# Third block's attention heads: the order of scores, transpositions and products, two heads apart

## The chip, the cores and the metric

The kernel runs on one core of a Trainium2 chip. The metric is the device time of one launch in microseconds (us), the median of several launches. Engines are named as in the profile: PE (TensorE, matrix products), DVE (VectorE), ACT (ScalarE), POOL (GpSimd), SP (the queue that starts most transfers).

## What is computed

The reference is a model of three parts on 256 tokens of width 1024: a retention layer and a sparse-attention layer, each followed by a mixture of experts, and then a block ("third block" in the kernel's order of stages) with two branches, a state-space branch and a dilated-window attention. The change touches only that attention, which has 12 heads of width 64; at this length each head's whole 256 x 256 matrix of scores is formed. Cut to what matters:

```python
scores = einsum('bdhine,bdhime->bdhinm', qs, ks) * (1.0 / sqrt(e))
scores = scores - slopes * dist          # dist is masked beyond the window
m = max(scores, axis=-1)
p = exp(scores - m)
den = sum(p, axis=-1)
o = einsum('bdhinm,bdhime->bdhine', p, vs) / den
lse = m + log(den)
```

In the same stretch of the program the input `xbc` of the state-space branch (3072 columns, 12 halves of a slab of 512 columns, 256 each) is projected, convolved over five taps and passed through silu. The two pieces of work are independent; the kernel pairs one attention head with one half-slab of `xbc`.

## The kernel before

The kernel is written engine by engine, each with its own instruction stream, and the order on an engine is the order of the code. Semaphores join them: `wait_ge` stands in an engine's stream and everything behind it on that engine waits too.

For one head `hd` the pieces are:

- S, the scores on PE (`att_scores`, matmul line L1204): two 64-row products into one bank of accumulation memory.
- L, on DVE: scores plus distance term into `a_S` (L2279), the largest value per row (L2283) and its scaled negative (L2284), which raises `att_max_ready`.
- E, on ACT: two exponentials with row sums (L1653) into `a_P`, which raise `att_exp_ready`.
- T, on PE: four 128 x 128 transpositions of `a_P` (`transpose4`, L853) into a bank; then the copy of that bank to `a_PT` by ACT (L1658).
- P, on PE: the products with the values (L1225) into a bank; then the copy to `a_o` by DVE (L2289).
- X, on PE: the projection of one half-slab of `xbc` (`xbc_half`, `split_columns`, 48 matmuls, L804). Weights are split in two parts: `high(q)` on ACT rounds a half-slab (L1407), `low(q)` on DVE forms the rest (L1829), and X waits for `low`. `high(q)` waits until PE has finished the half-slab two before it.
- On the side: ACT copies each finished pair of half-slabs to `c_raw` (L1666), DVE convolves (`conv(n)`, L2267 and L2269), ACT applies silu (`conv_out(n)`, L1645).

In the trace one f32 matmul of S or P stands as two rows (four rows for S, eight for P), one of T or X as one.

The four banks for such intermediate results are used in turn: bank number `b` may be taken when `b - 4` has been copied out (`take_aux`). On PE the loop before is, for each head, S, X, T, P. T waits for E of the same head, P for the copy of the transpositions, which begins when T ends.

Behind the 12 heads come the cumulative sums of the state-space branch (L1235, L1241) and the "gates" projection: four half-slabs, called G0 to G3 here, again L804. `high` of G2 waits for G0's end. Behind it, in the order of ACT and DVE, stand `low` of G2, the last convolution, `conv_out(11)`, the logarithm of the row sums (L1676), `high` and `low` of G3, and G3 waits for that.

Of the kernel before, what the change touches and what calls it, by code (L numbers as in the profile page):

```python
# [25 lines left out]
ACT = mybir.ActivationFunctionType  # L26
# [3 lines left out]
P = 128  # L30
T = 256
NT = T // P
# [20 lines left out]
NSA_H, NSA_G, DH = 16, 4, 64  # L53
# [5 lines left out]
ATT_H, ATT_PAT, ATT_HPP = 12, 3, 4  # L59
# [14 lines left out]
SL, PJ, AX, AR = {}, {}, {}, {}  # L74
# [77 lines left out]
def build(nc, x_tok, x_feat, slabs, experts_w, c_all, c_ret, c_nsa, c_ssd, c_att, w_pattn, ln_gb, out):  # L152
    ctx = ExitStack()
    with ctx:
# [378 lines left out]
        def wait_aux_out(eng, b):  # L533

            eng.wait_ge(aux_out[b % 4], b // 4 + 1)
# [17 lines left out]

        def nsa_ready(*name):
            return AR["nsa_att"] + NSA_BANK[name] + 1

        def aux(b):
            return bank(4 + b % 4)
# [212 lines left out]
        def _(pe):  # L771
# [9 lines left out]
            def take_aux(b):  # L781
                if b >= 4:
                    wait_aux_out(pe, b - 4)
                return aux(b)
# [64 lines left out]
            def transpose4(b, src):  # L849

                dst = take_aux(b)
                for q in range(4):
                    last = nc.tensor.transpose(dst[:, q * P:(q + 1) * P], src(q), ident)  # L853
                last.then_inc(aux_ready, 1)
# [343 lines left out]


            def att_scores(hd):  # L1200
                s = take_aux(AX["att"] + 3 * hd)
                half = slice(hd % 2 * DH, hd % 2 * DH + DH)
                for i in range(NT):
                    last = nc.tensor.matmul(s[:, i * T:(i + 1) * T], a_qkT[half, hd // 2, i * P:(i + 1) * P],  # L1204
                                            a_qkT[half, 6 + hd // 2, :], start=True, stop=True)
                last.then_inc(aux_ready, 1)

            def xbc_half(n):

                j = PJ["att"] + n // 2  # L1210
                split_columns(take_pair(j) if n % 2 == 0 else pair(j), HQ["att"] + n, a_hT)

            for s in (3, 4):
                wait_pair_out(pe, PJ["att_in"] + s)
            for hd in range(ATT_H):
                att_scores(hd)
                xbc_half(hd)
                b = AX["att"] + 3 * hd
                pe.wait_ge(att_exp_ready, hd + 1)
                transpose4(b + 1, lambda q: a_P[:, hd % 2, q * P:(q + 1) * P])  # L1220
                o = take_aux(b + 2)
                wait_aux_out(pe, b + 1)
                for i in range(NT):
                    for k in range(NT):
                        last = nc.tensor.matmul(o[:, i * DH:(i + 1) * DH],  # L1225
                                                a_PT[:, hd % 2, (2 * i + k) * P:(2 * i + k + 1) * P],
                                                a_v[:, k, hd * DH:(hd + 1) * DH], start=(k == 0), stop=(k == 1))
                last.then_inc(aux_ready, 1)


            TRI = ((tri_gt, 0, 0), (tri_le, 0, 1), (tri_ge, 1, 0), (tri_lt, 1, 1))
# [148 lines left out]
        def _(act):  # L1380
# [11 lines left out]
            def high(q):  # L1392

                n, half = SPLIT_SLABS[q // 2], q % 2
                if q == 0:
                    act.wait_ge(first_half, 16)
                elif q == 1:
                    act.wait_ge(slab_loaded[0], 16)
                elif half == 0:
                    act.wait_ge(slab_loaded[n % NSLOT], 16 * (n // NSLOT + 1))  # L1400
                    act.wait_ge(half_done, q // 2)
                    for layer, stage in enumerate(("nsa_in", "att_in")):
                        if q == HQ[stage]:
# [237 lines left out]
            def conv_out(n):  # L1641

                act.wait_ge(conv_ready, n + 1)
                for c in range(2):
                    last = nc.scalar.activation(xbcT[:, 2 * n + c, :], c_acc[:, n % 2, c, :], ACT.Silu,  # L1645
                                                bias=conv_b[:, 2 * n + c:2 * n + c + 1])
                last.then_inc(xbc_ready, 1)

            for hd in range(ATT_H):
                u = hd % 2  # L1650
                act.wait_ge(att_max_ready, hd + 1)
                for i in range(NT):
                    last = nc.scalar.activation(a_P[:, u, i * T:(i + 1) * T], a_S[:, u, i * T:(i + 1) * T], ACT.Exp,  # L1653
                                                bias=a_nmax[:, hd, i:i + 1], scale=DH ** -0.5, accum_out=a_den[:, hd, i:i + 1])
                last.then_inc(att_exp_ready, 1)
                b = 3 * hd + 1
                act.wait_ge(aux_ready, AR["att"] + b + 1)
                nc.scalar.activation(a_PT[:, u, :], aux(AX["att"] + b), ACT.Copy).then_inc(aux_out[(AX["att"] + b) % 4], 1)  # L1658
                high(HQ["att"] + hd + 2)
                if hd % 2:  # L1660
                    s = hd // 2
                    j = PJ["att"] + s
                    act.wait_ge(slab_done, SL["att"] + s + 1)
                    if s >= 2:
                        act.wait_ge(conv_ready, 2 * (s - 2) + 2)
                    nc.scalar.activation(c_raw[:, s % 2, :, 2:2 + T], pair(j).rearrange("p (c t) -> p c t", c=4),  # L1666
                                         ACT.Copy).then_inc(pair_out[j % 2], 1)
                if hd >= 3:
                    conv_out(hd - 3)
            conv_out(9)  # L1670
            high(HQ["gates"] + 2)
            conv_out(10)
            conv_out(11)

            act.wait_ge(att_o_ready, ATT_H)
# [138 lines left out]
        def _(dve):  # L1814
            link = chain(dve, dve_chain)
            V = nc.vector
# [9 lines left out]
            def low(q):  # L1826

                dve.wait_ge(w_high, q + 1)
                V.tensor_tensor(half_of(ring_low, q), half_of(ring, q), rounded_half(q).bitcast(F32),  # L1829
                                ALU.subtract).then_inc(w_low, 1)  # L1830
# [424 lines left out]
            def conv(n):  # L2255

                if n % 2 == 0:
                    wait_pair_out(dve, PJ["att"] + n // 2)
                if n >= 2:
                    dve.wait_ge(xbc_ready, n - 1)  # L2260
                for k in range(TAPS):
                    for c in range(2):
                        ch = 2 * n + c
                        tap = conv_w[:, ch * TAPS + k:ch * TAPS + k + 1]
                        src = c_raw[:, n // 2 % 2, 2 * (n % 2) + c, k:k + T]
                        if k == 0:
                            last = V.tensor_scalar(c_acc[:, n % 2, c, :], src, tap, None, ALU.mult)  # L2267
                        else:
                            last = V.scalar_tensor_tensor(out=c_acc[:, n % 2, c, :], in0=src, scalar=tap,  # L2269
                                                          in1=c_acc[:, n % 2, c, :], op0=ALU.mult, op1=ALU.add)  # L2270
                    if k < TAPS - 1:
                        link(last)
                last.then_inc(conv_ready, 1)

            dve.wait_ge(att_loaded, 16)
            for hd in range(ATT_H):
                u, b = hd % 2, AX["att"] + 3 * hd
                dve.wait_ge(aux_ready, AR["att"] + 3 * hd + 1)
                V.scalar_tensor_tensor(out=a_S[:, u, :], in0=a_dist[:, hd // ATT_HPP, :],  # L2279
                                       scalar=-(DH ** 0.5) * 2.0 ** (-8.0 * (hd + 1) / ATT_H), in1=aux(b),  # L2280
                                       op0=ALU.mult, op1=ALU.add).then_inc(aux_out[b % 4], 1)
                wait_aux_out(dve, b)
                link(V.tensor_reduce(a_max[:, hd, :], a_S[:, u, :].rearrange("p (i n) -> p i n", i=NT), AXX, ALU.max))  # L2283
                V.tensor_single_scalar(a_nmax[:, hd, :], a_max[:, hd, :], -DH ** -0.5, ALU.mult).then_inc(att_max_ready, 1)  # L2284
                if hd >= 2:
                    conv(hd - 2)
                low(HQ["att"] + hd + 2)
                dve.wait_ge(aux_ready, AR["att"] + 3 * hd + 3)
                V.tensor_copy(a_o[:, hd, :, :], aux(b + 2)[:, 0:NT * DH].rearrange("p (i d) -> p i d", i=NT)  # L2289
                              ).then_inc(aux_out[(b + 2) % 4], 1)  # L2290
            conv(10)
            low(HQ["gates"] + 2)
            conv(11)

            wait_aux_out(dve, AX["att"] + 3 * ATT_H - 1)
            V.engine_nop().then_inc(att_o_ready, ATT_H)
# [410 lines left out]
```

## Time and profile before

| | us |
|---|---|
| median of 3 runs | 1629.32 (1629.0 to 1632.28) |
| the profiled execution's own time | 1626.07 |
| its span, first to last instruction | 1624.3 |
| PE busy in the span | 1460.8 |
| DVE busy | 776.8 |
| ACT busy | 553.1 |
| first score matmul to the first matmul of G0 | 1030.17 to 1156.53 |

Times of the trace count from the start of the span. Busy shares are means over all stages; the stretch that the change touches is about 8% of the span. "PEclk" is the clock that TensorE was granted, as a share of 2.4 GHz; it is either 1.00 or 0.50 at any moment, and a figure between is a mean over the stretch.

### The profile page before, as it was taken

How to read it: one execution, taken by the hardware profiler on the slowest of the kernel's cores; microseconds unless marked ns; L12 is line 12 of the kernel's file. 1: busy time of each engine (PE TensorE's matmuls, PEld its weight loads, DVE VectorE, ACT ScalarE, POOL GpSimd, SP SyncE). 2: the span in 40 equal slices, each digit the busy share in tenths (PEclk: the TensorE clock that was granted, in tenths of full speed). 3: DMA queues.
4: the chain of work that ended last, by engine and by line, in shares of the span. 5: the costliest groups of instructions: out<-in, count | busy, mean ns of one | idle time of the engine just before them, and what ended most of it. 6: DMA issues, size and time to landing. Idle time of an engine off the chain costs nothing. (4 is left out here: it accounts for less than half of the span.)

```text
span 1624.3 us, 20275 instructions
## 1 busy us (share of the span) xinstructions
PE 1460.8 (90%) x8750; PEld 1098.9 (68%) x8750; DVE 776.8 (48%) x1030; ACT 553.1 (34%) x752; POOL 63.5 (4%) x73
## 2 busy tenths in 40 slices
PE   6999968999988989959999969799889899789996
PEld 6987755444436778754444439688877799689985
DVE  4646551221235647440222153478768874555544
ACT  3343421010103444211010013467646763334431
POOL 0000010000002000010000010000012100000000
PEclk9999977999997999959999979899989899989998
DMA  8543854999972520458999954333311224534550
GB/s 322 204 176 135 327 216 184 429 427 428 428 330 97 226 86 1 164 224 362 429 427 428 426 226 150 126 113 125 127 52 53 104 105 162 201 130 167 197 203 30
DMA packets 27602, 355.26 MB, mean 219 GB/s; under 512 B 2864, under 2 KB 4912, under 8 KB 5616
## 3 DMA queue, kind: packets, MB, share of 16 engines
q1 hardware_dynamic: 25696, 341.85, 52.6%
q0 software_dynamic: 1808, 12.01, 1.9%
q8 instruction: 73, 1.20, 0.3%
q14 instruction: 25, 0.20, 0.0%
HBM read 352.80 MB, written 1.05 MB: 218 GB/s over the span
## 5 line engine op out<-in xcount | busy, mean ns | idle before, releaser
L1829 DVE TENSOR_TENSOR ring_low<-ring,w_rounded 128x2048 fp32r<-128x2048 f32 (+1 forms) x128 | 291.4, 2277 | 317.6 <-ACT w_rounded L1407 309.7
L1407 ACT ACTIVATE w_rounded<-ring 128x2048 fp32r<-128x2048 f32 (+1 forms) x128 | 242.9, 1900 | 338.9 <-PE ps L804 125.2
L804 PE MATMUL ps<-split,w_rounded 128*128 128x256 f32 x1056 | 255.1, 292 | 24.5 <-DVE ring_low L1829 17.6
L804 PE MATMUL ps<-split,ring_low 128*128 128x256 f32 x800 | 232.0, 290 | 0.0
L804 PEld LDWEIGHTS ps<-split,w_rounded 128*128 128x128 f32 x1056 | 190.0, 198 | 30.2 <-issue 24.8
L818 PE MATMUL ps<-w_rounded,split 128*128 128x512 f32 (+1 forms) x448 | 156.4, 398 | 8.8 <-DVE ring_low L1829 2.9
L804 PE MATMUL ps<-hT_low,w_rounded 128*128 128x256 f32 x544 | 158.3, 291 | 0.0
L804 PEld LDWEIGHTS ps<-split,ring_low 128*128 128x128 f32 x800 | 158.1, 198 | 0.0
L818 PE MATMUL ps<-ring_low,split 128*128 128x512 f32 (+1 forms) x304 | 118.9, 391 | 0.0
L2044 DVE TENSOR_SCALAR split<-ps,work 128x1024 fp32r<-128x1024 f32 x16 | 20.5, 1284 | 197.1 <-PE ps L979 197.1
L804 PEld LDWEIGHTS ps<-hT_low,w_rounded 128*128 128x128 f32 x544 | 109.0, 200 | 0.0
L818 PEld LDWEIGHTS ps<-w_rounded,split 128*128 128x128 f32 x448 | 86.0, 192 | 28.7 <-issue 8.1
L842 PE MATMUL ps<-w_rounded,split 128*128 128x512 f32 x384 | 104.3, 392 | 0.0
L947 PE MATMUL ps<-work 128*64 128x512 f32 x448 | 100.3, 596 | 0.0
L947 PE MATMUL ps<-ring,work 128*64 128x512 f32 x416 | 93.8, 596 | 0.0
L2038 DVE TENSOR_TENSOR work<-work,ps 128x512 f32<-128x512 f32 x16 | 11.0, 688 | 157.1 <-PE ps L947 157.1
L842 PEld LDWEIGHTS ps<-w_rounded,split 128*128 128x128 f32 x384 | 71.9, 188 | 16.3 <-issue 0.7
L1492 ACT ACTIVATE work<-ps 128x512 f32<-128x512 f32 x16 | 9.6, 597 | 187.1 <-PE ps L967 187.1
L979 PE MATMUL ps<-work 128*64 128x512 f32 x320 | 70.5, 593 | 0.1
L947 PEld LDWEIGHTS ps<-work 128*64 128x64 f32 x448 | 30.7, 137 | 58.3 <-issue 58.3
L932 PE MATMUL ps<-split,split 128*128 128x128 f32 x256 | 64.8, 296 | 4.0 <-DVE split L2028 4.0
L818 PEld LDWEIGHTS ps<-ring_low,split 128*128 128x128 f32 x304 | 58.1, 191 | 12.0
(333 smaller groups left out, 2343.5 us busy)
## 6 DMA issues: line engine op xcount, KB each, us to landing
ring<-slabs SPq DMA_DIRECT2D x65, 2048.0 KB, 7.6
work<-experts_w SPq DMA_DIRECT2D x48, 2048.0 KB, 16.0
ring<-experts_w SPq DMA_DIRECT2D x36, 2048.0 KB, 14.3
w_plain<-experts_w SPq DMA_DIRECT2D x12, 2048.0 KB, 13.8
gb<-ln_gb POOLq DMA_DIRECT2D x6, 1024.0 KB, 7.9
ring<-slabs SPq DMA_DIRECT2D x2, 1024.0 KB, 9.5
hT<-x_feat SPq DMA_DIRECT2D x1, 1024.0 KB, 5.0
work<-c_ret POOLq DMA_DIRECT2D x1, 1024.0 KB, 11.8
```

The source lines that it names most:

```text
L804: last = nc.tensor.matmul(dst[:, at:at + T], w3[a][:, k, c * P:(c + 1) * P], src[b][:, k, :], start=(k == 0 and t == 0), stop=(k == KC - 1 ...
L818: last = nc.tensor.matmul(dst[:, i * 512:i * 512 + cols], src[a][:, 4 * half + k, i * P:(i + 1) * P], w3[b][:, k, :], start=(half == k == ...
L842: last = nc.tensor.matmul(dst[i][:, c * 512:(c + 1) * 512], src(a, s)[:, 2 * half + k, i * P:(i + 1) * P], w3[b][:, k, c * 512:(c + 1) * 512],
L932: nc.tensor.matmul(tok[:, k, :], h_[:, i, k * P:(k + 1) * P], m_S[:, i, :], start=(i == part == 0), stop=(i == part == 1))
L947: last = nc.tensor.matmul(bank(b)[e * CAP:(e + 1) * CAP, :], m_xT[:, e2 % 2, 4 * half + k, e * CAP:(e + 1) * CAP], w4[:, e, k, :], start=( ...
L979: last = nc.tensor.matmul(bank(4 + c)[e * CAP:(e + 1) * CAP, :], m_heT[:, 2 * half + k, e * CAP:(e + 1) * CAP], w4[:, e, k, c * 512:(c + 1 ...
L1407: nc.scalar.activation(rounded_half(q), half_of(ring, q), ACT.Copy).then_inc(w_high, 1)
L1492: nc.scalar.activation(m_heT.rearrange("p k s -> p (k s)"), bank(2), ACT.Copy).then_inc(ps_.heT_ready, 1)
L1829: V.tensor_tensor(half_of(ring_low, q), half_of(ring, q), rounded_half(q).bitcast(F32), ALU.subtract).then_inc(w_low, 1)
L2038: V.tensor_tensor(m_he, m_sg, bank(1), ALU.mult).then_inc(ps_.he_ready, 1)
L2044: V.tensor_scalar(high, bank(4, 2), m_w[:, e2:e2 + 1], None, ALU.mult).then_inc(ps_.weighed, 1)
```

## The change

All engines' orders are changed together, so that a head's scores, largest values and exponentials run two heads ahead. PE begins with S0, X0, S1, X1, and goes on with T, then S of two heads later, then P, then X of two heads later; the last two heads stand as T10, T11, P10, P11. The order in which the four banks are taken follows (`att_bank`). ACT begins with E0, `high`, E1; then for each head the copy of the transpositions, `high`, every second time `c_raw`, E of two heads later, `conv_out` of the head before. DVE begins with L0, L1, `low`; then for each head L of two heads later, the copy of the products, `low`, `conv` of the same head.

```diff
+        def att_bank(name, hd):
+            b = {"scores": 3 * hd - 3 if hd >= 2 else hd, "P": 3 * hd + 2 if hd <= 10 else 3 * hd,
+                 "o": 3 * hd + 4 if hd <= 10 else 3 * hd + 2}[name]
+            return AX["att"] + b
...
-            for hd in range(ATT_H):
-                att_scores(hd)
-                xbc_half(hd)
...
+            for hd in range(2):
+                att_scores(hd)
+                xbc_half(hd)
+            for hd in range(ATT_H - 2):
+                att_transposes(hd)
+                att_scores(hd + 2)
+                att_products(hd)
+                xbc_half(hd + 2)
+            for hd in (ATT_H - 2, ATT_H - 1):
+                att_transposes(hd)
+            for hd in (ATT_H - 2, ATT_H - 1):
+                att_products(hd)
...
+            att_exps(0)
+            high(HQ["att"] + 2)
+            att_exps(1)
+            for hd in range(ATT_H):
+                b = att_bank("P", hd)
+                act.wait_ge(aux_ready, att_bank_ready("P", hd))
+                nc.scalar.activation(a_PT[:, hd % 2, :], aux(b), ACT.Copy).then_inc(aux_out[b % 4], 1)
+                if hd < ATT_H - 1:
+                    high(HQ["att"] + hd + 3)
+                if hd % 2 == 0:
...
+                if hd + 2 < ATT_H:
+                    att_exps(hd + 2)
+                if hd:
+                    conv_out(hd - 1)
             high(HQ["gates"] + 2)
-            conv_out(10)
             conv_out(11)
...
+            att_largest(0)
+            att_largest(1)
+            low(HQ["att"] + 2)
+            for hd in range(ATT_H):
+                if hd + 2 < ATT_H:
+                    att_largest(hd + 2)
+                b = att_bank("o", hd)
+                dve.wait_ge(aux_ready, att_bank_ready("o", hd))
+                V.tensor_copy(a_o[:, hd, :, :], aux(b)[:, 0:NT * DH].rearrange("p (i d) -> p i d", i=NT)
+                              ).then_inc(aux_out[b % 4], 1)
+                if hd < ATT_H - 1:
+                    low(HQ["att"] + hd + 3)
+                conv(hd)
+                if hd == ATT_H - 2:
+                    low(HQ["gates"] + 2)
```

The order on PE around one head in the middle, before (L853 is T, L1225 is P, L1204 is S, L804 is X; the semaphores that a row waits for stand behind it):

```order
L804 MATMUL ps<-split_27680_76,ring_low 128x256
L853 MATMUL ps<-call,work 128x128 [waits aux_out0,att_exp_ready]
L853 MATMUL ps<-call,work 128x128 x3
L1225 MATMUL ps<-work 128x64 [waits aux_out0,aux_out1]
L1225 MATMUL ps<-work 128x64 x3
L1204 MATMUL ps<-work 128x256 [waits aux_out2]
L1204 MATMUL ps<-work 128x256
L804 MATMUL ps<-split_27680_76,w_rounded 128x256 [waits w_low]
```

And in the changed kernel, where the same lines are numbered L861, L1232, L1212 and L812:

```order
L812 MATMUL ps<-split_27680_76,ring_low 128x256
L861 MATMUL ps<-call,work 128x128 [waits aux_out1,att_exp_ready]
L861 MATMUL ps<-call,work 128x128 x3
L1212 MATMUL ps<-work 128x256 [waits aux_out2]
L1212 MATMUL ps<-work 128x256
L1232 MATMUL ps<-work 128x64 [waits aux_out1,aux_out3]
L1232 MATMUL ps<-work 128x64 x3
L812 MATMUL ps<-split_27680_76,w_rounded 128x256 [waits w_low,pair_out0]
```

The scores moved from behind the products to between transpositions and products.

The end of the heads on PE in the changed kernel (L1255 and L1261 are the cumulative sums, then G0 begins):

```order
L861 MATMUL ps<-call,work 128x128 [waits aux_out1,att_exp_ready]
L861 MATMUL ps<-call,work 128x128 x3
L861 MATMUL ps<-call,work 128x128 [waits aux_out2,att_exp_ready]
L861 MATMUL ps<-call,work 128x128 x3
L1232 MATMUL ps<-work 128x64 [waits aux_out1,aux_out3]
L1232 MATMUL ps<-work 128x64 x3
L1232 MATMUL ps<-work 128x64 [waits aux_out2,aux_out0]
L1232 MATMUL ps<-work 128x64 x3
L1255 MATMUL ps<-work 128x32 [waits a_ready,aux_out1]
L1255 MATMUL ps<-work 128x32 x3
L1261 MATMUL ps<-work 96x128 [waits copies_ready,aux_out2]
```

The last two heads now stand together, with no half-slab between them, and the last products wait for the copy of the last transpositions (`aux_out2`).

What ACT does between the copies of those two heads in the changed kernel (L1683 is the copy, L1427 `high`, L1692 `c_raw`, L1665 `conv_out`; before, one copy and one `high` stood there per head, and E after them):

```order
L1683 ACTIVATE work<-ps 128x512 [waits aux_ready]
L1427 ACTIVATE w_rounded<-ring 128x2048 [waits slab_done]
L1692 ACTIVATE work<-ps 128x4x256 [waits conv_ready,slab_done]
L1665 ACTIVATE work<-work 128x256 [waits conv_ready]
L1665 ACTIVATE work<-work 128x256
L1683 ACTIVATE work<-ps 128x512 [waits aux_ready]
```

Between the last two copies stand a `high`, a `c_raw` and the two instructions of `conv_out(9)`.

## Rows read from the trace of the kernel before

**Rows 1.** Page, busy time of each engine: us, share of the span, instructions.

```profile
PE 1460.8 (90%) x8750; PEld 1098.9 (68%) x8750; DVE 776.8 (48%) x1030; ACT 553.1 (34%) x752; POOL 63.5 (4%) x73
```

**Rows 2.** Waits of PE, 1027 to 1200 us: total, times, longest.

```profile
PE ps L1225 <- ACT work L1658: 9.3, 12, 0.8
PE ps L853 <- ACT work L1653: 6.2, 1, 6.2
```

**Rows 3.** Timeline of PE, heads 0 and 1: start, duration, engine, line, count.

```profile
1030.17 1.10 PE L1204 MATMUL ps<-work 64*128 64x256 f32 x4 [2.59 <-issue]
1031.20 0.39 PE L804 MATMUL ps<-split,w_rounded 128*128 128x256 f32 x1
...
1043.40 1.11 PE L853 MATMUL ps<-call,work 128*128 128x128 f32 x4 [6.21 <-ACT work L1653]
1047.16 2.07 PE L1204 MATMUL ps<-work 64*128 64x256 f32 x4
1056.79 0.60 PE L853 MATMUL ps<-call,work 128*128 128x128 f32 x4
```

**Rows 4.** Timeline of PE, heads 2 and 3.

```profile
1066.06 0.60 PE L853 MATMUL ps<-call,work 128*128 128x128 f32 x4
1067.44 1.07 PE L1225 MATMUL ps<-work 128*128 128x64 f32 x8 [0.78 <-ACT work L1658]
1068.44 1.13 PE L1204 MATMUL ps<-work 64*128 64x256 f32 x4
1075.34 0.60 PE L853 MATMUL ps<-call,work 128*128 128x128 f32 x4
```

**Rows 5.** Timeline of ACT, head 3.

```profile
1075.97 0.60 ACT L1658 ACTIVATE work<-ps 128x512 f32<-128x512 f32 x1 [1.71 <-PE ps L853]
1076.46 1.90 ACT L1407 ACTIVATE w_rounded<-ring 128x2048 fp32r<-128x2048 f32 x1
1078.27 1.02 ACT L1666 ACTIVATE work<-ps 128x1024 f32<-128x1024 f32 x1
1079.30 1.28 ACT L1645 ACT_TABLE_LOAD   x1
1080.60 0.91 ACT L1645 ACTIVATE work<-work 128x256 f32<-128x256 f32 x2
...
1083.73 0.19 ACT L1653 ACTIVATION_READ_ACCUMULATOR work<-work 128x1 f32 x1
```

**Rows 6.** Timeline of DVE, heads 2 and 3.

```profile
1069.12 2.29 DVE L1829 TENSOR_TENSOR ring_low<-ring,w_rounded 128x2048 fp32r<-128x2048 f32 x1 [1.08 <-ACT w_rounded L1407]
1071.34 0.28 DVE L2289 COPY work<-ps 128x128 f32<-128x128 f32 x1
...
1078.40 2.29 DVE L1829 TENSOR_TENSOR ring_low<-ring,w_rounded 128x2048 fp32r<-128x2048 f32 x1 [1.08 <-ACT w_rounded L1407]
```

**Rows 7.** Timeline of ACT, the first exponentials.

```profile
1040.95 1.28 ACT L1653 ACT_TABLE_LOAD   x1 [5.06 <-DVE work L2284]
...
1043.15 0.19 ACT L1653 ACTIVATION_READ_ACCUMULATOR work<-work 128x1 f32 x1
```

**Rows 8.** Timeline of PE, last products and first matmul of G0.

```profile
1153.91 1.08 PE L1225 MATMUL ps<-work 128*128 128x64 f32 x8 [0.78 <-ACT work L1658]
...
1156.53 0.37 PE L804 MATMUL ps<-split,w_rounded 128*128 128x256 f32 x1
```

**Rows 9.** Windows: stretch, us, PE busy (matmuls), PEclk, DMA share, GB/s.

```profile
1040.00:1042.50 2.50, 0.00 (x0) 0.50 0.00 0
...
1097.50:1100.00 2.50, 2.50 (x13) 0.53 1.00 426
1100.00:1102.50 2.50, 2.50 (x19) 0.79 0.24 98
...
1145.00:1147.50 2.50, 2.50 (x13) 0.58 0.00 0
```

**Rows 10.** Timelines of ACT and DVE, `high` of G2 and `low` of G3.

```profile
1162.60 1.92 ACT L1407 ACTIVATE w_rounded<-ring 128x2048 fp32r<-128x2048 f32 x1 [3.10 <-PE ps L804]
...
1175.35 2.29 DVE L1829 TENSOR_TENSOR ring_low<-ring,w_rounded 128x2048 fp32r<-128x2048 f32 x1 [1.18 <-ACT w_rounded L1407]
```

More of the change, by code:

```diff
@@ L555, in nsa_ready, with att_bank_ready @@
             return AR["nsa_att"] + NSA_BANK[name] + 1
+        def att_bank(name, hd):
+            b = {"scores": 3 * hd - 3 if hd >= 2 else hd, "P": 3 * hd + 2 if hd <= 10 else 3 * hd,
+                 "o": 3 * hd + 4 if hd <= 10 else 3 * hd + 2}[name]
+            return AX["att"] + b
+        def att_bank_ready(name, hd):
+            return AR["att"] + att_bank(name, hd) - AX["att"] + 1
         def aux(b):
@@ L1200, in att_scores @@
             def att_scores(hd):
-                s = take_aux(AX["att"] + 3 * hd)
+                s = take_aux(att_bank("scores", hd))
                 half = slice(hd % 2 * DH, hd % 2 * DH + DH)
@@ L1214, in _, with att_transposes, att_products @@
                 wait_pair_out(pe, PJ["att_in"] + s)
-            for hd in range(ATT_H):
-                att_scores(hd)
-                xbc_half(hd)
-                b = AX["att"] + 3 * hd
+            def att_transposes(hd):
                 pe.wait_ge(att_exp_ready, hd + 1)
-                transpose4(b + 1, lambda q: a_P[:, hd % 2, q * P:(q + 1) * P])
-                o = take_aux(b + 2)
-                wait_aux_out(pe, b + 1)
+                transpose4(att_bank("P", hd), lambda q: a_P[:, hd % 2, q * P:(q + 1) * P])
+            def att_products(hd):
+                o = take_aux(att_bank("o", hd))
+                wait_aux_out(pe, att_bank("P", hd))
                 for i in range(NT):
@@ L1647, in conv_out, with att_exps @@
                 last.then_inc(xbc_ready, 1)
-            for hd in range(ATT_H):
+            def att_exps(hd):
                 u = hd % 2
@@ L1655, in _ @@
                 last.then_inc(att_exp_ready, 1)
[L1656 to L1660, printed above, removed]
+            att_exps(0)
[8 more added lines that the diff above has]
+                if hd % 2 == 0:
                     s = hd // 2
@@ L1667, in _ @@
                                          ACT.Copy).then_inc(pair_out[j % 2], 1)
-                if hd >= 3:
-                    conv_out(hd - 3)
-            conv_out(9)
+                if hd + 2 < ATT_H:
+                    att_exps(hd + 2)
+                if hd:
+                    conv_out(hd - 1)
             high(HQ["gates"] + 2)
-            conv_out(10)
             conv_out(11)
@@ L2275, in _, with att_largest @@
             dve.wait_ge(att_loaded, 16)
-            for hd in range(ATT_H):
-                u, b = hd % 2, AX["att"] + 3 * hd
-                dve.wait_ge(aux_ready, AR["att"] + 3 * hd + 1)
+            def att_largest(hd):
+                u, b = hd % 2, att_bank("scores", hd)
+                dve.wait_ge(aux_ready, att_bank_ready("scores", hd))
+                if hd >= 2:
+                    dve.wait_ge(att_exp_ready, hd - 1)
                 V.scalar_tensor_tensor(out=a_S[:, u, :], in0=a_dist[:, hd // ATT_HPP, :],
@@ L2284, in _ @@
                 V.tensor_single_scalar(a_nmax[:, hd, :], a_max[:, hd, :], -DH ** -0.5, ALU.mult).then_inc(att_max_ready, 1)
[L2285 to L2293, printed above, removed]
+            att_largest(0)
[13 more added lines that the diff above has]
+                    low(HQ["gates"] + 2)
             wait_aux_out(dve, AX["att"] + 3 * ATT_H - 1)
```

## The prediction

> **What bounds the kernel now.** I read the busy times first: PE is busy in 90% of the span [rows 1], so anything that lets PE start its next matmul earlier can count, and other engines matter where PE waits for them. Then I asked for PE's waits in the stretch of the attention heads. Two kinds stand out [rows 2]: twelve waits, 9.3 us together, of the products (P) for ACT's copy of the transpositions (T), and one of 6.2 us of the first T for the first exponentials (E). The timeline says why. In a head in the middle P starts 1.38 us after T, 0.78 of it idle, because ACT can only begin its copy when T has ended; the scores (S) follow 1.00 us after P, and 6.90 us later comes the next T, so a head takes 9.28 us [rows 4]. In head 0 PE runs out of work after S0 and X0 (1030.17 + 6.90 = 1037.07) and stands until 1043.40 [rows 3]; E0 ends only at 1043.34 [rows 7].
>
> The windows view adds a cost that no wait shows. During that stall the granted clock falls to 0.50, that is 1.2 GHz instead of 2.4 [rows 9]. From T0 at 1043.40 to T1 at 1056.79 pass 13.39 us [rows 3] where a head takes 9.28 [rows 4]: 4.1 us lost to the clock. The clock fell twice more for a short time, right behind a group T, P, S: 0.53 and 0.79 in two neighbouring windows of 2.5 us [rows 9], which is 0.47 x 2.5 + 0.21 x 2.5 = 1.7 us of full speed lost, and again from 1145 [rows 9].
>
> The other two engines have little room. DVE goes from one `low` to the next in 9.28 us, with 1.08 idle [rows 6]: 8.20 us of work per head. ACT, in a head with `c_raw`, works from 1075.97 to 1083.73 + 0.19 without a gap: 7.95 us; in the others 1.03 less [rows 5].
>
> **The change, step by step.** No instruction is added or removed; bytes and transfers are the same, and no transfer is moved past another on a queue. Only waits and the clock can change the time. I work in the times of the trace before, at full clock first.
>
> Start. S takes 1.03 us start to start [rows 3], so X takes 6.90 - 1.03 = 5.87. PE now does S0, X0, S1, X1: 1030.17 + 2 x 6.90 = 1043.97. That is 0.6 us after E0 ends, so the wait of 6.2 us disappears. Here T0 starts, then S2 (0.45 + 1.03, to 1045.45; the 0.45 is an estimate, as T's four rows last 0.60 and P's overlap with the next matmul is 0.07, S's 0.1 [rows 3, 4]; 0.60 is its upper bound, 0.15 a head). P0 needs ACT's copy, and ACT has E0 (to 1043.34), `high` (1.81 start to start [rows 5]) and E1 (1.10, the time from the table load's end to the last row [rows 7]) before it: the copy starts at 1043.34 + 1.81 + 1.10 = 1046.25, and P starts 0.75 after a copy starts (T to P 1.38 [rows 4] less T to copy 0.63 [rows 4, 5]), at 1047.00. So a new wait of 1.55 us stands before P0. X2 starts at 1048.00; its weights' `low` follows `high` (1045.15) and is done about 1047.5. T1 starts at 1053.87.
>
> Steady state. A period is now T 0.45, S 1.03, P 1.00, X 5.87 = 8.35 us. P can start 1.38 after T at the earliest and comes 1.48 after it, so the copy is hidden by S with 0.1 to spare. DVE needs 8.20, ACT 7.95 at most: both fit, with 0.15 and 0.4 us. I checked who is queued behind whom: L of two heads later can start 1.6 us after T (S ended) and DVE comes free from `conv` about then; E of two heads later is wanted a whole period later; `low` has a period of slack; banks are free one step ahead. If the cover goes, each us by which DVE or ACT exceeds 8.35 costs 9 us over the nine periods. T10 starts at 1053.87 + 9 x 8.35 = 1129.0.
>
> End. T10 and T11 stand together, P10 starts after 1.38. The copy for P11 is queued on ACT behind `high` of G1, `c_raw` and `conv_out(9)`: 1129.0 + 0.63 + 0.49 + 1.81 + 1.03 + 0.92 = 1133.9 (each start to start in [rows 5]), so P11 starts at 1134.65, and PE is idle about 3.2 us between P10 and P11, a wait that was 0.78 before. `conv(9)`, which `conv_out(9)` needs, ends near 1130.5 (8.2 a head after the one before it), so it isn't late. From P11 to G0 are 2.62 us [rows 8]: G0 starts at 1137.3 against 1156.53 [rows 8], which is 19.2 us earlier.
>
> Behind it. From G0's end runs a chain: `high` of G2 starts at once when G0 ends, and `low` of G3 starts 12.75 us later [rows 10]; its members are the same in the changed kernel, except that DVE's copy of the last products stands in front of the last convolution, 0.2 us more (it is 0.28 long and partly overlapped [rows 6]). G3 waits for this chain in both. All later stages hang on it, none of them on a transfer that runs by its own time here (in this stretch DMA rests for whole windows [rows 9]), so the shift should arrive at the end: -19.0 us.
>
> Clock. The 19.0 contains the clock losses of before (4.1 + twice 1.7) as gone, since the changed kernel's steady state has no gap in its T, S, P group. Two new gaps can bring a loss. The one at the end (3.2 us idle between short matmuls, 8 us without an X) lies between a short fall's 1.7 and the first stall's 4.1 [rows 3, 9]; I take 3.6, nearer to the stall of 6.21, because the light work around the gap lasts as long. For the gap of 1.55 before P0 the bounds are 0 and 1.7: I take 1.5, since it is longer than the 0.78 gaps, two of which ended in a fall. Together 5.1.
>
> Sum: -19.0 + 5.1 = -13.9 us. The profiled execution took 1626.07, so 1612.2 for one like it; the median of the runs shown is 3.25 above that execution, which gives 1615.4.
>
> On ACT's table loads the traces and the notes part. A switch between exp and silu costs 1.30 us from the load's start to the next activation [rows 5], twice a head, before and after. The Trainium skill (ScalarE: Activation LUTs, section "What ACT_TABLE_LOAD costs") adds a drain to the load and arrives at 2.66 us a switch. By that, ACT would need 2.7 us more a head than rows say, 10.2 on the average, and the changed kernel would be bound by ACT. The trace doesn't agree: the activation starts 0.02 us after the load's end.
>
> **The rivals.**
> 1. The schedule holds and the clock never falls at the gaps: 19.0 gained, 1610.3. For it: 2.59 us of idle before S0 left the following matmuls fast (X0's first rows, S 1.03) [rows 3]. Against it: the end has a longer poor stretch. 15%.
> 2. DVE becomes the bound. Its margin is 0.15 us of 8.35, and each of its small waits for PE's S or ACT's `c_raw` would come on top. With 0.7 us a head more the gain falls by 9 x 0.55 = 5 us, to about 1620.5; with PE's old period kept (0.93 a head, 8.4 us) to 1623.8. Against it: `low` and `conv` are started by work that is done a step ahead. 17%.
> 3. The clock costs more than I took: both gaps at the long price (4.1 each) and 2 us more in G0: 1620.5. 9%.
> 4. The other side: ACT becomes the bound. It is one mechanism: in the new order E, silu and the time-critical copy are queued in one row, and if each of two table switches a head took twice its 1.30 us, ACT would need 7.43 + 2.6 = 10.0 us on the average, 1.7 more than PE, over nine periods 15 us: 1615.4 + 15 = 1630.4, no gain, and slower if anything is added. It decides from 9.9 us a head on. Against it: 7.95 measured without a gap, in the same mix. By the skill's figure of that page it would be some 17 us and 1632. 3%.
> 5. The time is given back later: G3's chain or the state-space stage turns out to be paced by something that did not move. Then 0 to -3: 1626 to 1629. For it nothing in the views; 3%.
>
> **How the numbers follow.** My forecast has 53%: 1615.4, by itself 1612.5 to 1618. With rivals 1 to 3, which together hold 41%, the range goes from 1609.5 to 1622.5; the unknown price of the clock alone is 0 to 8.2 us around 5.1. About 0.2% (3.3 us) is what a measurement of this kernel can tell from no change. Faster by more than that are forecast and rivals 1 to 3, and a little of 5: 0.94. Same: most of 5 and half of 4, 0.04. Slower: 0.02.
>
> **What would show it.** PE's wait for the first E gone, and one of about 1.5 us before P0 in its place; no idle before P in heads 1 to 9; T to T 8.35 us; one wait of about 3.2 us before the last P; G0 19 us less the clock's losses after S0 than before (107 instead of 126 us at full clock); PEclk at 0.5 behind the last P and 1.0 in heads 2 to 9. If T to T is near 8.2 or below, or DVE has no idle left while PE waits, rival 2 is at work. I would be wrong above all if the clock behaves otherwise in the T, S, P groups.

## The result

The changed kernel takes 1609.03 us (median of 4, 1607.97 to 1610.41), the kernel before in the same comparison 1630.02: ratio 0.987, 95% interval 0.9853 to 0.9887. It is faster by 21.0 us. Forecast were 13.9 us and 1615.4, and the median lies 0.5 us below the low end of the range. A second comparison (below) gave 1609.89 against 1628.44, ratio 0.9895 (0.9872 to 0.9917), 18.6 us. The profiled execution went from 1626.07 to 1607.97, 18.1 us.

First the page of the changed kernel, where PE's row and the span answer to [rows 1]:

```profile
span 1606.2 us, 20285 instructions
PE 1454.3 (91%) x8750; PEld 1094.4 (68%) x8750; DVE 777.2 (48%) x1030; ACT 552.8 (34%) x752; POOL 64.4 (4%) x73
```

DVE and ACT work as long as before; only PE's own busy time fell a little, 1460.8 to 1454.3. Most of that fits the matmuls that no longer run at the lower clock (7.1 us lost to the clock in this stretch before, 1.6 after, both worked out below). The waits of PE, 1027 to 1180 us, against [rows 2]:

```profile
PE ps L1232 <- ACT work L1683: 4.3, 3, 2.9
PE ps L1289 <- DVE work L2394: 4.0, 1, 4.0
PE ps L812 <- DVE ring_low L1855: 3.9, 1, 3.9
```

The wait for the first exponentials (6.2 us) is gone, and of twelve waits before the products three are left. The wait before G3 (L812, the gates projection) is 3.9 us where it was 3.7, as forecast. Where they are shows PE's timeline (T is L861 here, S L1212, P L1232; the half-slabs between them are left out), against [rows 3, 4, 8]:

```profile
1030.53 1.10 PE L1212 MATMUL ps<-work 64*128 64x256 f32 x4 [2.59 <-issue]
...
1044.43 0.60 PE L861 MATMUL ps<-call,work 128*128 128x128 f32 x4
1044.96 1.13 PE L1212 MATMUL ps<-work 64*128 64x256 f32 x4
1047.12 1.08 PE L1232 MATMUL ps<-work 128*128 128x64 f32 x8 [1.03 <-ACT work L1683]
1053.81 0.60 PE L861 MATMUL ps<-call,work 128*128 128x128 f32 x4
1054.34 1.13 PE L1212 MATMUL ps<-work 64*128 64x256 f32 x4
1055.39 1.10 PE L1232 MATMUL ps<-work 128*128 128x64 f32 x8
...
1062.14 0.60 PE L861 MATMUL ps<-call,work 128*128 128x128 f32 x4
...
1128.81 1.03 PE L861 MATMUL ps<-call,work 128*128 128x128 f32 x8
1130.19 1.08 PE L1232 MATMUL ps<-work 128*128 128x64 f32 x8 [0.34 <-ACT work L1683]
1134.18 1.08 PE L1232 MATMUL ps<-work 128*128 128x64 f32 x8 [2.92 <-ACT work L1683]
1135.09 1.49 PE L1255 MATMUL ps<-work 128*128 128x32 f32 x8
1136.39 2.00 PE L1261 MATMUL ps<-work 128*96 128x128 f32 x8
1138.04 0.56 PE L812 MATMUL ps<-split,w_rounded 128*128 128x256 f32 x1
```

A reader can lay this beside the schedule of the prediction, counted from S0: T0 13.90 (forecast 13.80), P0 16.59 (16.83) behind a wait of 1.03 (1.55), T1 23.28 (23.70), T to T 8.33 (8.35), T10 98.28 (98.8), P11 103.65 (104.5) behind a wait of 2.92 (3.2), G0 107.5 (107.1 at full clock). From the first scores to G0 were 126.4 us in the profiled execution before. Behind G0 little changed in sum: 35.25 us to the next long join, L1289 at 1173.29, where L1269 (the same join in the kernel before) came 35.67 us after G0, at 1192.20.

The clock is what came out otherwise. Windows of PE, with the granted clock in the third figure from the right:

```profile
1045.00:1047.50 2.50, 1.47 (x9) 1.00 0.80 216
...
1132.50:1135.00 2.50, 0.82 (x8) 1.00 1.00 419
1135.00:1137.50 2.50, 2.50 (x16) 0.60 0.25 95
1137.50:1140.00 2.50, 2.50 (x18) 0.72 0.00 0
```

No fall at the gap before P0, and one short fall that begins right behind P11, in the cumulative sums (L1255 takes 1.49 us where L1235 took 1.03), and is over some matmuls into G0. From P11 to G0 pass 3.86 us instead of 2.62, and about 0.4 is lost in G0 (21.75 us from G0 to G3, 21.17 before with a wait 0.2 shorter): 1.6 us in all.

### The profile page after: what moved, and what is told of

Same layout as the page of the kernel before. It is cut to its first block and busy times, and to the rows that moved or that the text cites. A ratio compares the mean times of both kernels' runs of the same rounds, so it can differ in the third digit from the quotient of the medians.

```text
span 1606.2 us, 20285 instructions
## 1 busy us (share of the span) xinstructions
PE 1454.3 (91%) x8750; PEld 1094.4 (68%) x8750; DVE 777.2 (48%) x1030; ACT 552.8 (34%) x752; POOL 64.4 (4%) x73
## 3 DMA queue, kind: packets, MB, share of 16 engines
HBM read 352.80 MB, written 1.05 MB: 220 GB/s over the span
## 5 line engine op out<-in xcount | busy, mean ns | idle before, releaser
L1427 ACT ACTIVATE w_rounded<-ring 128x2048 fp32r<-128x2048 f32 (+1 forms) x128 | 242.9, 1900 | 341.5 <-PE ps L812 128.6
L812 PE MATMUL ps<-split,w_rounded 128*128 128x256 f32 x1056 | 253.8, 290 | 24.2 <-DVE ring_low L1855 17.4
L812 PE MATMUL ps<-split,ring_low 128*128 128x256 f32 x800 | 230.2, 288 | 0.0
L812 PEld LDWEIGHTS ps<-split,w_rounded 128*128 128x128 f32 x1056 | 188.5, 196 | 26.3 <-issue 20.7
L812 PEld LDWEIGHTS ps<-split,ring_low 128*128 128x128 f32 x800 | 156.1, 195 | 0.0
L812 PE MATMUL ps<-hT_low,w_rounded 128*128 128x256 f32 x544 | 155.8, 286 | 0.0
L812 PEld LDWEIGHTS ps<-hT_low,w_rounded 128*128 128x128 f32 x544 | 106.7, 196 | 0.0
L955 PEld LDWEIGHTS ps<-work 128*64 128x64 f32 x448 | 30.7, 137 | 58.3 <-issue 58.3
## 6 DMA issues: line engine op xcount, KB each, us to landing
w_plain<-experts_w SPq DMA_DIRECT2D x12, 2048.0 KB, 13.9
```

The source lines that it names most:

```text
L812: last = nc.tensor.matmul(dst[:, at:at + T], w3[a][:, k, c * P:(c + 1) * P], src[b][:, k, :], start=(k == 0 and t == 0), stop=(k == KC - 1 ...
L955: last = nc.tensor.matmul(bank(b)[e * CAP:(e + 1) * CAP, :], m_xT[:, e2 % 2, 4 * half + k, e * CAP:(e + 1) * CAP], w4[:, e, k, :], start=( ...
```

## Experiments

Each was timed against the kernel before, in three groups, each on one chip. The changed kernel is in the first group only (the first four runs). Where a later run is set against its 1609.89 us, the comparison goes across groups and chips; the kernel before took 1628.44, 1628.15 and 1630.28 us in the three, so a difference of 2 us of that kind is not shown by the times alone.

**The two kernels again.** No edit. First the kernel before.

> The kernel before, unchanged, timed against itself: a ratio of 1.000 within 0.2%. It is there for its second profiled execution. If the 2.9 us by which the medians' difference (21.0) exceeds the difference of the two profiled executions (18.1) comes from short falls of the granted clock that differ between executions, the stretch from the first scores to G0 is longer here than 126.4 us, with more or longer falls behind the groups of transpositions, products and scores. If it comes from elsewhere, that stretch is again within 1 us of 126.4 and other stretches are longer.

Measured: 1628.34 against 1628.44, ratio 0.9998 (0.9984 to 1.0012). The second profiled execution does differ from the first in the stretch that matters: G0 starts 130.0 us after the first scores (1160.75 - 1030.71), not 126.4. Its windows show why:

```profile
1117.50:1120.00 2.50, 2.50 (x14) 0.73 1.02 433
1120.00:1122.50 2.50, 2.50 (x15) 0.59 0.52 216
...
1127.50:1130.00 2.50, 2.50 (x13) 0.78 0.00 0
1130.00:1132.50 2.50, 2.50 (x14) 0.54 0.00 0
...
1150.00:1152.50 2.50, 2.50 (x14) 0.50 0.00 0
...
1160.00:1162.50 2.50, 2.50 (x14) 0.50 1.03 439
```

With the fall from 1097.5 that both traces have, four groups T, P, S ended in a fall here, two in the first trace. Each such head is 10.8 us long (1125.35 to 1136.11 from T to T, for one) where the others take 9.3, so a fall costs 1.5:

```profile
1125.35 0.60 PE L853 MATMUL ps<-call,work 128*128 128x128 f32 x4
...
1136.11 0.60 PE L853 MATMUL ps<-call,work 128*128 128x128 f32 x4
```

A fifth fall stands behind the last products, whose gap is 0.78 us too (the window from 1160). P11 to G0 took 3.19 us there instead of 2.62, and G0 to G3 took 1.0 us more than in the first trace. So the kernel before loses 7.1 us to the clock up to G0 in one profiled execution (4.1 in head 0, twice 1.5) and about 10.7 in the other (4.1, four times 1.5, 0.6). Then the changed kernel:

> The changed kernel, unchanged, as the measure for the other runs of this chip: about 21 us (1.3%) faster than the kernel before. Its trace should again show T to T in 8.33 us, the clock at full speed from the first scores to the tenth products, and one fall at the last products that costs 1 to 2 us up to G0 and 0.5 in G0. If the lucky side of the clock explains the first trace, this one shows a fall behind P0 or a longer one at the end, up to 4 us.

Measured: 1609.89. Its trace repeats the first: G0 107.49 us after the first scores (107.51), the same single fall. The changed kernel's loss to the clock here was the same in both.

**Scores behind the products, two heads ahead.**

```diff
-                att_scores(hd + 2)
                 att_products(hd)
+                att_scores(hd + 2)
```

(with the bank numbers `3 * hd - 2` for scores and `3 * hd + 3` for products)

> As the changed kernel, but the scores of two heads ahead stand behind the products again (order T, P, S, X; banks numbered to match); scores, largest values and exponentials still run two heads ahead. Theory one (standing between T and P, the scores hide the copy): the wait of 0.78 us before the products is back in every head, T to T 9.27 us instead of 8.33, so 9 x 0.94 = 8.5 us slower than the changed kernel, and the clock falls come back behind some of the groups, 1.5 us each: 1618 to 1622. The first wait of 6.2 us stays away. Rival (running ahead alone is what pays, since every wait is shorter when its input is early): T to T stays at 8.3 to 8.6 us, within 3 us of the changed kernel.

Measured: 1624.77, ratio to the kernel before 0.9974 (0.9959 to 0.9988). Most of the gain is gone though every head still runs two ahead:

```profile
PE ps L1232 <- ACT work L1683: 12.4, 12, 2.9
...
1066.20 0.60 PE L861 MATMUL ps<-call,work 128*128 128x128 f32 x4
1067.58 1.08 PE L1232 MATMUL ps<-work 128*128 128x64 f32 x8 [0.78 <-ACT work L1683]
1068.59 1.13 PE L1212 MATMUL ps<-work 64*128 64x256 f32 x4
1075.49 0.60 PE L861 MATMUL ps<-call,work 128*128 128x128 f32 x4
...
1147.50:1150.00 2.50, 1.16 (x6) 0.54 0.97 413
...
1155.00:1157.50 2.50, 2.50 (x14) 0.50 0.00 0
```

The wait of 0.78 is back in each head and T to T is 9.29 us. The rival falls: running ahead alone does not shorten the wait for the copy, since the copy can't begin before T ends. The stretch to G0 is 14.0 us longer than in the changed kernel (121.47 to 107.49): 9 x 0.95 = 8.5, the gap before P0 now 2.12 us (1.1 more), two falls behind groups (3.0), and P11 to G0 5.06 us instead of 3.84 (1.2). The two falls are the other half of the lesson: with the 0.78 gap in the group they are back, while heads 1 to 9 have no fall in any of the eleven traces in which the scores stand between. The last term comes from the gap of 2.92 us before P11, which is the changed kernel's. Here the clock fell about 1.1 us before P11 began, inside the gap, and came back 10 us later, in G0. By the rows from P11 to G0 (5.06) and from G0 to G3 (23.11) that cost 4.2 us, where the changed kernel lost 1.6.

**One head ahead.** On all engines the lead is one head; the scores stand between T and P.

```diff
-            for hd in range(2):
-                att_scores(hd)
-                xbc_half(hd)
-            for hd in range(ATT_H - 2):
-                att_transposes(hd)
-                att_scores(hd + 2)
-                att_products(hd)
-                xbc_half(hd + 2)
...
+            att_scores(0)
+            xbc_half(0)
+            for hd in range(ATT_H):
+                att_transposes(hd)
+                if hd + 1 < ATT_H:
+                    att_scores(hd + 1)
+                att_products(hd)
+                if hd + 1 < ATT_H:
+                    xbc_half(hd + 1)
```

> The scores stand between T and P, but only one head ahead on all engines: S0, X0, then T, S of the next head, P, X of the next head. Theory one: T to T is 8.33 us as in the changed kernel, since the copy is hidden all the same, but the first T again waits 6.2 us for the first exponentials and the clock falls there at a cost of about 4 us; the last head waits for its copy 0.78 us only, not 2.9. Sum against the changed kernel: +6.2 - 1.0 (the wait before P0) + 4 - 2.5 (the end) - 1.8 (its clock fall) = about 5 us slower, 1614. Rival (two heads of lead are needed for DVE and ACT to keep up): waits for the exponentials or for the low parts appear in every head, T to T above 8.6 us, 1618 or more.

Measured: 1615.72, ratio 0.992 (0.9901 to 0.9939), 5.8 us above the changed kernel where 5 were expected. T to T is 8.33, one head of lead is enough for DVE and ACT; the first wait is back with its fall:

```profile
1044.12 1.11 PE L861 MATMUL ps<-call,work 128*128 128x128 f32 x4 [6.21 <-ACT work L1670]
1045.17 2.07 PE L1212 MATMUL ps<-work 64*128 64x256 f32 x4
...
1056.92 0.60 PE L861 MATMUL ps<-call,work 128*128 128x128 f32 x4
```

T0 to T1 is 12.80 us where 8.33 would do: 4.5 us to the clock. There is no gap of 2.9 us at the end either: P11 waits 0.78 us, and no fall comes there. The two runs thus separate what the change did: the place of the scores takes away the gap per head and the falls behind the groups; the second head of lead takes away the wait at the start, with its fall, and brings the gap before P11.

**The copy of the last transpositions first.** ACT copies the banks of heads 10 and 11 one behind the other.

```diff
             for hd in range(ATT_H):
+                if hd < ATT_H - 1:
+                    att_copy(hd)
+                if hd == ATT_H - 2:
+                    att_copy(hd + 1)
```

> The changed kernel, but ACT copies the last transpositions right behind the tenth head's, ahead of the rounding of G1, c_raw and conv_out(9). Theory (the wait before the last products is ACT's queue order, and the clock's fall there follows from it): P11 follows P10 with at most 0.2 us of idle, 2.9 us gained, and the fall of the clock at P11 (1.2 us up to G0, 0.5 in G0) is gone too: 4.6 us, 1605 where the changed kernel has 1609.9. Rival one: the clock falls all the same, since T10, T11, P10, P11 and the cumulative sums are short matmuls in a row: 2.9 us. Rival two: conv(10) and conv_out(10), which are now behind by one copy, delay the rounding of G2 and take part of it back: under 2 us.

Measured: 1604.84, ratio 0.9855 (0.984 to 0.9871), 5.1 us better than the changed kernel's 1609.89 (across groups), and 23.3 better than the kernel before in its own. P11 follows P10 without a gap, no fall comes at G0, and G0 starts 103.21 us after the first scores:

```profile
1130.87 1.97 PE L1232 MATMUL ps<-work 128*128 128x64 f32 x16 [0.34 <-ACT work L1683]
...
1133.54 1.09 PE L1261 MATMUL ps<-work 128*96 128x128 f32 x8
```

So the gap at the end was ACT's queue order. The fall is gone with it in this trace, but that it followed from the gap is not shown. Three traces below (all three together, and the early rounding with this copy) have no gap before P11 and yet a fall of 3.4 us in the cumulative sums, which is what the rival expected of short matmuls in a row.

**The third rounding ahead of the first exponentials.**

```diff
+            high(HQ["att"] + 2)
             att_exps(0)
-            high(HQ["att"] + 2)
             att_exps(1)
```

> The changed kernel, but ACT rounds the third half-slab before the first exponentials, in the 5 us in which it waits for the largest values. Theory: the first exponentials aren't later, the copy of the first transpositions starts as soon as they end, the wait of 1.03 us before P0 goes: 1 us gained, at the edge of what is measurable, and the clock has no fall here before or after. Rival: the rounding runs into the first exponentials and pushes T0: 1 us or more lost.

Measured: 1612.46, ratio 0.9904 (0.9889 to 0.9919), 2.6 us above the changed kernel's 1609.89 (across groups; the interval of the ratio overlaps the one that goes with that time, 0.9872 to 0.9917), though the edit did what it should: P0 at 1046.43 follows S2 without a wait, and T10 comes 97.24 us after S0 instead of 98.28. Neither theory has it; the rival's time came, but not by its mechanism, since T0 isn't pushed (13.90 us after S0, as in the changed kernel). The loss stands at the other end of the heads:

```profile
1129.56 1.08 PE L1232 MATMUL ps<-work 128*128 128x64 f32 x8 [0.34 <-ACT work L1683]
1133.56 1.94 PE L1232 MATMUL ps<-work 128*128 128x64 f32 x8 [2.92 <-ACT work L1683]
...
1132.50:1135.00 2.50, 1.44 (x7) 0.50 0.98 419
1135.00:1137.50 2.50, 2.50 (x14) 0.50 0.04 10
...
1140.00:1142.50 2.50, 2.50 (x14) 0.50 0.00 0
```

The same gap of 2.9 us comes 1 us earlier, the clock falls inside it, and comes back only in G0, about 10 us later. P11 to G0 take 5.06 us instead of 2.62 and G0 to G3 1.8 more than at full clock: 4.2 us lost instead of 1.6, the same as with the scores behind the products.

**The last convolution ahead of the low part of G2.** On DVE `conv(11)` comes before `low` of G2; on ACT `conv_out(11)` and the logarithm before its rounding.

```diff
                 conv(hd)
-                if hd == ATT_H - 2:
-                    low(HQ["gates"] + 2)
...
                           ALU.subtract).then_inc(att_mix_ready, 1)
+            low(HQ["gates"] + 2)
             low(HQ["gates"] + 3)
```

> The changed kernel, but on DVE the last convolution stands ahead of the low part of G2, and on ACT conv_out(11) and the logarithm of the row sums ahead of the rounding of G2. DVE is idle there for 8.1 us. Theory (the wait of 3.9 us before G3 is this queue order, and its clock fall follows from it): the wait is gone, the fall of about 2.4 us too, 6 us gained. Rival one: the gain of 6 us is taken back at the next join, where PE waits 4.0 us for DVE's copy behind the low part of the state-space weights, since DVE's chain after G3 is as long as before: 0 to 2 us. Rival two: G2 is late now, as its rounding waits behind the logarithm: slower.

Measured: 1603.94, ratio 0.985 (0.9837 to 0.9864), 5.95 us better than the changed kernel's 1609.89 (across groups), and 24.2 better than the kernel before in its own. The wait of 3.9 before G3 is gone; from G0 to L1289 pass 29.84 us instead of 35.28. The wait of 4.0 at that join is still there, but moved forward with everything else, so nothing was taken back.

**All three together.**

> The three edits of the other runs together. If each theory holds and they are independent, 4.6 + 1.0 + 6 = 11.6 us faster than the changed kernel, 1598. If conv(10) sets the time of the last convolution, the last_conv part loses what the tail part gains, since G0 starts earlier and DVE doesn't: 1602 or so.

Measured: 1604.4, ratio 0.9864 (0.9843 to 0.9885): no better than either of the two large edits by itself. G0 starts 4.9 us earlier after the first scores than with the last convolution alone (102.6 for 107.5), but ACT's logarithm, which stands behind DVE's last convolutions and their `conv_out`, only 0.6 (113.9 for 114.5). So G2's rounding (1146.45), which stands behind it, and its low part are late, and PE waits there. The fall behind the last products is there too, with no gap before P11 (3.4 us at half speed from 1134.0).

```profile
PE ps L812 <- DVE ring_low L1861: 3.0, 1, 3.0
...
1144.10 0.91 ACT L1665 ACTIVATE work<-work 128x256 f32<-128x256 f32 x2 [3.48 <-DVE work L2301]
...
1146.45 3.69 ACT L1427 ACTIVATE w_rounded<-ring 128x2048 fp32r<-128x2048 f32 x2
```

**The two large edits, put together rightly.** ACT as in the changed kernel but for the early copy; on DVE `low` of G2 stands behind the last convolution and ahead of the wait for the logarithm.

```diff
             V.engine_nop().then_inc(att_o_ready, ATT_H)
+            low(HQ["gates"] + 2)
```

> The changed kernel with ACT's copy of the last transpositions right behind the tenth head's, and on DVE the last convolution ahead of the low part of G2, but that low part ahead of the wait for the logarithm; ACT rounds G2 ahead of conv_out(11), as in the changed kernel. In the run with all three edits G2 had become late (3.0 us), because its rounding and low part stood behind the logarithm. Theory: here they don't, so both gains add: 5.0 + 5.9 us, 1599. Rival: the chain conv(10), last convolution, logarithm sets the start of G3 and only moves the wait there: 1603 to 1605.

Measured: 1599.57 (1599.24 to 1601.46), ratio 0.9806 (0.9788 to 0.9823): 30.7 us better than the kernel before in the same group, and 10.3 below the changed kernel's time in the first group. Both gains add: G0 103.21 us after the first scores, L1289 29.80 after G0. It beats both kernels.

**The early rounding again, where no gap stands at the end.** Once with the early copy alone, once with the best version.

> The changed kernel with the early copy of the last transpositions and the third half-slab rounded ahead of the first exponentials. The copy alone gave 1604.8. Theory of the clock as above: no gap before the last products, no long fall, so the early rounding gives its 1.05 us: 1603.8. If the early rounding by itself is harmful as it looked (2.6 us slower than the changed kernel): 1607.

Measured: 1604.92, ratio 0.9856 (0.9832 to 0.988), against 1604.84 without the rounding.

> The run before it, with the third half-slab rounded ahead of the first exponentials as well. If the rounding itself costs nothing and the 2.6 us lost by that edit alone came from the clock at the last products (10 us at half speed there instead of 3.5), then here, where no gap stands before the last products, it gains its 1.05 us: 1598. If the edit itself costs something, 1600 or more.

Measured: 1599.71, ratio 0.9811 (0.979 to 0.9832), against 1599.57. The loss of 2.6 us is gone in both, so the rounding by itself does no harm that shows. Its 1.05 us aren't there either: in both traces a fall of 3.4 us now begins during the cumulative sums that neither kernel had without the edit. The first:

```profile
1132.50:1135.00 2.50, 2.50 (x14) 0.50 0.90 380
```

It costs about 1.5 us in the first trace (0.5 before G0, 1.0 by G3), no less than the edit gives. The medians can't tell such amounts: two of the first kernel's five runs took over 1611 us.

**Everything from P0 on later.** ACT's copy of the first transpositions three times over.

> The changed kernel with ACT's copy of the first transpositions done three times over, so that everything from P0 on comes 1.2 us later and nothing else differs. In the traces of the changed kernel the clock falls at 1135.3, just after P11 has begun (1134.2), and is back after 3.4 us; with the early rounding it fell at 1132.3, in the gap ahead of P11, and was back after 10.3. Theory (what the fall costs depends on whether it comes before or after P11 starts): P11 now starts after 1135.3, the fall comes in the gap and lasts 7 to 10 us, 2 to 3 us more than in the changed kernel on top of the 1.2: 1613. Rival (the price of the fall doesn't depend on the place): 1611.1.

Measured: 1616.58, ratio 0.9902 (0.988 to 0.9923), 6.7 us above the changed kernel's 1609.89, but 13.7 better than the kernel before in its own group; the changed kernel was 18.6 better in the first group. The test is not the one that was planned. In its profiled execution the clock had already fallen at S0 and X0 took 3 us longer, so T0 was late and the longer copy was partly hidden (a gap of 0.98 before P0). Two other things stand in the trace:

```profile
1033.08 2.04 PE L1213 MATMUL ps<-work 64*128 64x256 f32 x4 [2.59 <-issue]
1049.95 0.60 PE L862 MATMUL ps<-call,work 128*128 128x128 f32 x4
1052.59 1.17 PE L1233 MATMUL ps<-work 128*128 128x64 f32 x8 [0.98 <-ACT work L1688]
...
1052.50:1055.00 2.50, 2.41 (x15) 0.69 0.95 400
1055.00:1057.50 2.50, 2.50 (x16) 0.63 0.72 308
...
1142.50:1145.00 2.50, 2.50 (x13) 0.50 0.04 10
...
1147.50:1150.00 2.50, 2.50 (x17) 0.70 0.00 0
```

First, the clock fell behind the gap before P0, which it did at none of the gaps of 1.03 to 1.07 us in five other traces: T0 to T1 is 10.85 us where the changed kernel has 9.38 and 9.45, so that fall costs 1.4 to 1.5. Second, the fall at the end began 1.0 us after P11 had started (1141.17), nearly as in the changed kernel (1.3), but lasted 6.8 us instead of 3.4 and cost 3.2 us (P11 to G0 4.14, G0 to G3 23.02). So "before or after P11 starts" does not decide the price by itself. Over all traces with the gap of 2.9 us, a fall that began 1.3 us after P11 started lasted 3.4 us (the changed kernel twice, the last convolution), one at 1.0 us after it 6.8, and those about 1.1 us before it 10.2 (two traces). The order fits a price that depends on the place, but no run moved the place alone.

## Why the prediction was right and where it was wrong

- **What bounded PE in the stretch.** Right: the wait for the copy, the wait for the first exponentials, the clock. The two variants of the order show each part's share.
- **Start, steady state, end.** Right within 0.9 us over 104 us. T to T was 8.33 for 8.35, in part by luck: T takes 0.53 start to start for 0.45, and P 0.92 for 1.00. The gap before P0 was 1.03 for 1.55: P0 came 0.24 earlier, mostly because the second exponentials took 0.98 us for 1.10 and the `high` ahead of them began 0.08 sooner, and the scores before it ended 0.28 later. At full clock the changed kernel would have reached G0 in 106.3 us (107.51 less 1.24), 0.9 less than forecast.
- **DVE and ACT fit into the shorter period.** Right; PE waits for neither in heads 1 to 9, and on ACT the activation behind a table load still starts 1.30 us after the load's start (1068.52 to 1069.82, for one). Rivals 2 and 4 fell.
- **Behind it.** Right: what G0 gained stood at the next join undiminished, 19.3 us (1192.20 - 1030.17 to 1173.29 - 1030.53). Of it 18.1 arrive at the end of the span: S0 comes 0.4 later, and behind the join 0.8 is given back. Rival 5, which gave back nearly everything, fell.
- **Clock, the step that failed.** The mechanism was right, the size wrong. The step "Together 5.1" took 3.6 for the gap at the end and 1.5 for the one before P0; measured are 1.6 and 0, 3.5 us less. Neither trace of the changed kernel has a fall at P0, nor has the run with 2.12 us of gap there; the run with the first copy three times over has one, at 1.4 to 1.5 us, so the term has a price but not in every execution. The price of a short fall, 1.7 from the means of two windows, is 1.5 by the rows (T to T 10.80 for 9.28). For the end the bounds 1.7 and 4.1 were nearly right: 1.6 in the changed kernel, and 3.2 and 4.2 in variants with the same gap. I took the upper half where the lower came, and no run shows a reason by which the lower could have been foreseen. Rival 3, a dearer clock, fell.
- **From one execution to the median, the second step that failed.** "The median of the runs shown is 3.25 above that execution" was carried over from the kernel before to the changed one, whose median is 1.1 above its profiled execution, 2.2 us less (1.6 above in the second comparison). The offset belongs at least in part to the kernel before. Its groups T, P, S end in a fall in two heads of one execution and in four of another, 126.4 or 130.0 us for the stretch, and with the fall in G0 that is 4.6 of the 5.6 us between these two executions. The changed kernel, without the gap in the group, took 107.5 both times. Taking the falls away is worth more against the median than against the execution I had in hand. Two executions of each kernel show this; they do not measure how often the falls come.
- Both errors have one sign, and so has the schedule's: 3.5, 2.2 and 0.9 us against the 6.4 us by which the time was missed (1615.4 to 1609.03); smaller shifts before S0 and behind G0 nearly cancel. The low end of the range, 1609.5, stood only 0.8 us below rival 1's 1610.3, so it left no room for an error in the offset. Rival 1, no fall at either gap, came nearest, though there was one fall.

## What to carry to other kernels

Work that doesn't need the copy belongs between the producer and the consumer of a copy; running further ahead doesn't replace it. One head of lead hid the copy as well as two; the second was worth the wait at the start. When a loop is pipelined, look at its last turns separately: here the drained pipeline left the critical copy behind three others in ACT's queue, and moving it was worth 5 us. And take the clock's price from several executions: a saving that rests on falls that come and go should be stated with that spread.

## What was not expected of the hardware

- The granted clock falls behind a group of small matmuls with a gap of only 0.78 us in it in some heads and not in others, at varying heads from one execution to the next (two, four and two of the heads in three traces, 1.5 us each). In the nine groups of heads 1 to 9 without the gap it never did, in eleven traces.
- A gap is not needed for a fall among small matmuls. In all four traces with the early rounding the clock falls 101.5 to 101.6 us after the first scores (by windows of 0.5 us): in one the gap of 2.9 us lies there, in three the cumulative sums do, with no idle before P11. The traces with the early copy and without the early rounding have no fall there.
- The same gap of 2.9 us before P11 cost 1.6, 3.2 or 4.2 us, for falls of 3.4, 6.8 and 10.2 us. Single gaps of 1.03 to 2.12 us before P0, with scores just ahead, brought no fall in six traces, and one of 0.98 us did in a seventh. What sets the moments of the falls stays open; so does whether one microsecond saved early can be kept, since none of the four kernels in which it was saved shows the gain.
